# Two state buffers, the last batch's outputs ahead of the first early GLU products, and feature loads on two queues at the end of an S5 mixer

## The reference

```
bu = einsum('blgp,gnp->blgn', u, b_bar)            # 64 groups of 16 channels, 64 complex states each
_, states = associative_scan(..., (a_seq, bu))     # x_t = Abar x_{t-1} + Bbar u_t
y = real(einsum('blgn,gpn->blgp', states, c_mat)) + d * u
g = gelu(y.reshape(bsz, length, D_MODEL))
return (g @ w_glu_a) * sigmoid(g @ w_glu_b)
```

## Time and profile before

| | |
|---|---|
| median of 3 runs | 1217.22 us (1213.07 to 1218.24) |
| profiled execution | 1218.4 us |
| its span in the trace | 1215.6 us |
| mean granted PE clock | 0.969 of full speed |
| PE busy | 1149.1 us, 95% of the span |
| DVE, ACT, POOL busy | 566.5, 410.0, 199.9 us |

### The profile page before, as it was taken

One profiled execution on the slowest core, in us unless ns is written; L12 is line 12 of the kernel. 1 busy time (PEld: TensorE's weight loads), 2 busy tenths in 40 slices (PEclk: granted clock), 3 DMA queues, 4 the chain that ended last, 5 costly groups with the idle time before them and its releaser, 6 DMA issues.

```text
span 1215.6 us, 20049 instructions
## 1 busy us (share of the span) xinstructions
PE 1149.1 (95%) x8147; PEld 1027.3 (85%) x8147; DVE 566.5 (47%) x833; ACT 410.0 (34%) x698; POOL 199.9 (16%) x181
## 2 busy tenths in 40 slices
PE   4488889999999999999999989999999999999997
PEld 4376789999999999999999866668888888888886
DVE  5788743554344333334444345545443433444443
ACT  5723222332222222223332355543332322323332
POOL 3989700002111211100000000000211112110000
PEclk9997679999999999999999999989999999999999
DMA  7224332232223232222223311113233332323222
GB/s 133 73 61 104 85 88 93 82 105 70 90 84 104 69 103 88 76 70 95 95 89 110 110 48 36 36 35 104 76 97 104 104 95 79 102 74 95 95 96 90
DMA packets 119384, 104.58 MB, mean 86 GB/s; under 512 B 21868, under 2 KB 117216, under 8 KB 119008
## 3 DMA queue, kind: packets, MB, share of 16 engines
q1 hardware_dynamic: 108968, 99.58, 26.9%
q10 hardware_dynamic: 10368, 4.33, 1.5%
HBM read 98.11 MB, written 5.24 MB: 85 GB/s over the span
## 4 chain that ended last, share of the span: by engine, by line
issue 43%; PE 43%; POOL 6%; DVE 4%; ACT 1%; DMA 1%; SPq 0%; ACTq 0%; POOLq 0%; DVEq 0%
PE banks L1267 39%; POOL gate L551 2%; PE banks L1384 1%; PE banks L1379 1%; DMA raw_c_re<-in_ssm_c_re 1%; ACT u_row L608 1%; POOL read L513 0%; POOL read L508 0%; POOL read L510 0%; POOL read_t L512 0%; POOL read L511 0%; POOL read_t L509 0%; POOL turn L494 0%; PE banks L1341 0%; PE banks L1328 0%
## 5 line engine op out<-in xcount | busy, mean ns | idle before, releaser
L573 ACT CAST w_high<-raw 128x1024 fp32r<-128x1024 f32 x188 | 197.1, 1049 | 587.2 <-PE banks L1267 587.2
L872 DVE TENSOR_TENSOR w_low<-raw,w_high 128x1024 fp32r<-128x1024 f32 x188 | 230.6, 1227 | 215.2 <-ACT w_high L573 215.0
L1267 PE MATMUL banks<-x_high,w_high 128*128 128x512 f32 (+2 forms) x1184 | 321.8, 324 | 1.0 <-DVE x_low L1082 1.0
L1267 PE MATMUL banks<-x_high,w_low 128*128 128x512 f32 (+2 forms) x1184 | 319.5, 323 | 0.0
L1267 PE MATMUL banks<-x_low,w_high 128*128 128x512 f32 (+2 forms) x1184 | 318.3, 322 | 0.0
L1267 PEld LDWEIGHTS banks<-x_high,w_high 128*128 128x128 f32 x1184 | 199.8, 190 | 19.6 <-issue 2.0
L1267 PEld LDWEIGHTS banks<-x_low,w_high 128*128 128x128 f32 x1184 | 199.6, 189 | 16.2
L1267 PEld LDWEIGHTS banks<-x_high,w_low 128*128 128x128 f32 x1184 | 198.8, 189 | 16.5
L551 POOL TENSOR_TENSOR gate<-gate,rstd_row 128x528 f32<-128x528 f32 (+1 forms) x44 | 79.2, 1800 | 391.5 <-ACT gate L752 391.5
L1267 PE MATMUL banks<-a_high,w_high 128*128 128x256 f32 (+2 forms) x528 | 140.4, 320 | 0.0
L1267 PE MATMUL banks<-a_high,w_low 128*128 128x256 f32 (+2 forms) x528 | 140.2, 320 | 0.0
(11 more groups left out here) (268 smaller groups left out, 1227.4 us busy)
## 6 DMA issues: line engine op xcount, KB each, us to landing
raw<-in_ffn_w_gate SPq DMA_DIRECT2D x22, 1024.0 KB, 5.3
raw<-in_ffn_w_up SPq DMA_DIRECT2D x22, 1024.0 KB, 5.3
raw<-in_ffn_w_down SPq DMA_DIRECT2D x16, 768.0 KB, 4.3
raw<-in_ffn_w_down SPq DMA_DIRECT2D x16, 640.0 KB, 4.1
raw<-in_attn_w_qkv SPq DMA_DIRECT2D x6, 1024.0 KB, 5.0
raw<-in_ssm_w_glu_b SPq DMA_DIRECT2D x4, 1024.0 KB, 5.1
raw<-in_ssm_w_glu_a SPq DMA_DIRECT2D x4, 1024.0 KB, 5.5
k_toep<-k_dram SPq DMA_DIRECT2D x64, 64.0 KB, 2.2
```

The lines of the kernel that those rows point to most:

```text
L573: nc.scalar.copy(w_high[:, j], raw[:, slot, :, j * P:(j + 1) * P]).then_inc(w_rounded, 1)
L872: nc.vector.tensor_tensor(w_low[:, j], raw[:, slot, :, j * P:(j + 1) * P], w_high[:, j], ALU.subtract).then_inc(w_split, 1)
L1267: ins = nc.tensor.matmul(banks[:, bank + h, b0:b0 + cn], w[:, j, k, :], xx[:, first_k + k, c0 + base:c0 + base + cn], start=start and k == ...
```

## The change

`state` gets two buffers, used in turn, and DVE waits for the outputs of two batches ago in place of those of the last one. `outputs(7)` comes directly behind `outputs(6)` in PE's program; `early_glu(0)` comes behind it. Of the eight loads that bring back the last batch's features, ACT issues four and SP the other four. SP's four stand between the two loads of the second set of GLU weights (`i == 1`), and wait for the last store (`y_stored`) and for the `y_feat` buffer to be free (`gt_split`).

```
-        state = sb("state", [P, 2, PB, CS], scope=s5)
+        state = sb("state", [P, 2, 2, PB, CS], scope=s5)
...
                 load_tile(i, 0, by_rows(w_glu_b[0])[:, :, 2 * P * i:2 * P * (i + 1)], wait=i > 0)
+                if i == 1:
+                    b = BATCHES - 1
+                    sp.wait_ge(y_stored, 16 * BATCHES)
+                    sp.wait_ge(gt_split, b - 1)
+                    for g in range(GB // 2, GB):
+                        sp.dma_start(y_feat[g * GROUP:(g + 1) * GROUP, b % 2],
+                                     y_dram[b, :, :, g, :].rearrange("s q c -> q s c")).then_inc(y_placed, 16)
                 load_tile(i, 1, by_rows(w_glu_a[0])[:, :, 2 * P * i:2 * P * (i + 1)], wait=i > 0)
...
-                for g in range(GB):
+                for g in range(GB if b < BATCHES - 1 else GB // 2):
                     nc.scalar.dma_start(y_feat[g * GROUP:(g + 1) * GROUP, b % 2],
...
-                v, cross, out = state_banks(), zt[:].rearrange("p i r c -> p i (r c)"), state[:].rearrange("p i r c -> p i (r c)")
+                v, cross, out = state_banks(), zt[:].rearrange("p i r c -> p i (r c)"), state[:, b % 2].rearrange("p i r c -> p i (r c)")
...
-                if b >= 1:
-                    dve.wait_ge(y_ready, b)
+                if b >= 2:
+                    dve.wait_ge(y_ready, b - 1)
...
-                                                   state[hs, i, r_, :], start=False, stop=i == 1)
+                                                   state[hs, b % 2, i, r_, :], start=False, stop=i == 1)
...
                     injection(b + 1)
                     lags(b + 1)
                     additions(b + 1)
-                else:
-                    early_glu(0)
                 outputs(b)
+            early_glu(0)
             pe.wait_ge(state_ready, BATCHES)
             early_glu(1)
```

## The result

The changed kernel takes 1219.03 us in the median of 20 runs (1216.16 to 1222.76), the kernel before 1216.60 us in 20 (1213.07 to 1219.15). The ratio is 1.0020, with a 95% interval of 1.0011 to 1.0029: slower by 2.4 us (1.3 to 3.5). The prediction had +2.5 us and 1219.7 us. Of the executions behind the ratios further down two are left out, one of the kernel before at 1247.82 us (mean granted clock 0.883) and one of the version with the state ahead of the splits at 1610.46 us (0.665). The profiled execution of the changed kernel has a span of 1215.9 us, 0.3 us above that of before. Two single executions say less here than the medians: between block 2 and the end there are 1029.6 us after (1215.9 - 186.34) and 1034.0 us before (1215.6 - 181.56).

The account below looks back on a forecast made before the run. PE, busy for 95% of the span, was taken as the bound. +1.0 + 2.3 - 0.3 + 0 - 0.5 = +2.5 us gave 1220.9 us profiled, 1219.7 us for the median; range 1213.5 to 1224.5 us.

Parts of the forecast that it names:

- The state buffers: DVE's wait before writing `state` in the mixer goes, 5.6 us in all; worth 0, with bounds of 0 and -0.25 us.
- The wait ahead of `outputs(7)`: Between `outputs(6)` and `outputs(7)` PE idles for state 7, ready at 160.46: 3.5 us of PE time lost.
- `outputs(7)` at the low clock: Behind the idle gap `outputs(7)` takes 8.41 us and ends at 168.9, +1.0 us; other bound 4.67 us.
- 42 pairs: GLU products between `outputs(7)` and `k` = 7, 24 before: 11.8 us (10.3 to 12.0), 3.5 us low; `k` = 7 at 180.7.
- The data: Batch 7's data for `k` = 7 is ready at 176.4, 4.3 us before PE needs it; the two queues are worth nothing.
- Block 2: PE's start of GLU block 2, behind `k` = 7 and 3.16 us of sigmoid, cast and split: 184.6, +3.0 us.
- The clock term: Low clock in block 2 loses 0.9 us (0 to 1.7), where it lost 1.4 before: -0.5 us.
- the clock rising within `outputs(7)`: Rival: `outputs(7)` is low for 3.9 us, then fast, ending at 166.9; -1 us with the clock term, 1216.2 us; chance 0.14.
- the clock that doesn't come back: Rival: the 42 pairs all run low, 18.5 us; block 2 at 191.9, +10.3 us, about 1227 us; chance 0.06.
- late data: Rival: SP's loads, issued beside ACT's, land late, beyond the 4.3 us cover before `k` = 7; about 1220 to 1222 us; chance 0.06.

Follow-up runs that it names:

- the version with the state ahead of the splits: The full change with DVE's splits of the first two weight blocks moved behind the last batch's state: ratio 1.0000, 0.0 us against the kernel before.
- the twice-done `k`: The full change with `k` = 0 to 3 of the first GLU product also done, thrown away, between `outputs(6)` and `outputs(7)`: 1.0000, 0.0 us against before.
- the version that was clearly faster: The full change with state 7 before the weight splits, last Toeplitz blocks and gelu early on ACT, early products of blocks 0 and 1 interleaved: 0.9964, -4.4 us against before.
- the old order with buffers and queues: The full change with `early_glu(0)` put back ahead of `outputs(7)`, two state buffers and two queues kept: 0.9975, -3.0 us against the kernel before.

## Why the prediction was right

The direction, the size and the place were right: PE runs dry ahead of `outputs(7)` and is the bound from there. Step by step:

- *The state buffers.* Costed at 0, with a bound of -0.25 us. Their time alone, -1.3 us (-3.3 to +0.6), doesn't tell 0 from the bound, but at POOL the bound was too narrow: the trace has -1.7 us. It counted only POOL's wait of 0.25 us, and not the 0.84 us at 120.48, which is of the same kind and went too. In the full change they gave nothing: POOL's stretch was 74.5 us, not 73.6.
- *The wait ahead of `outputs(7)`.* Predicted 3.5 us, measured 7.42 in the trace. The size differs by the end of `outputs(6)`, which is early when the clock is high. The end of the wait, which is what counts, was predicted at 160.5 and came at 161.15. `k_toep` was expected at 157.3 and landed at 159.4; it doesn't bind only because the state is later still.
- *`outputs(7)` at the low clock.* 8.41 us predicted, 8.38 measured; it ended at 169.5, not 168.9. Here the Trainium skill ("TensorE: Matmul & The Clock Gate", Part 1) has sustained work release the low clock. The seven microseconds at 0.50 with PE busy throughout, from 162 to 169, again don't bear that out for these matmuls; the products of the twice-done `k` do bear it out.
- *42 pairs.* 11.8 us predicted, 12.95 measured (169.53 to 182.48), since the clock stayed low for 5.7 us and not 3.5; my bound of 12.0 was too tight.
- *The data.* Predicted 4.3 us ahead of PE, measured 5.2. The two queues are hidden in the full change, as said. Where PE waits for the data, the prediction gave them up to 1.84 us; the trace of the queues alone has 1.56 us, and its time, -1.5 us, doesn't exclude zero.
- *Block 2.* Predicted at 184.6, measured at 186.34, +4.8 us against before in these two traces. The clock term behind it was put at -0.5 us and was -1.4, since the clock didn't fall: the windows from 176 to 183 and from 186 to 195 us have 1.00. In the prediction's own terms the trace has +1.6 (end of `outputs(7)`) + 3.5 (42 pairs) - 0.3 - 1.4 (clock) = +3.4 us, where the sum had +1.0 + 2.3 - 0.3 - 0.5 = +2.5; the times give 2.4 (1.3 to 3.5). That the sum hit the median so closely is partly luck: each term was off by 0.6 to 1.2 us, two of them one way and one the other, and one trace's clock pattern isn't the mean of them.

Of the rivals, the clock rising within `outputs(7)`, the clock that doesn't come back, and late data are all absent from the trace.

## What to carry to other kernels

Before moving a step up in an engine's program, read when its inputs are ready, and what the work that it jumps over was covering: here the 18 pairs of products were free filling for a state that came no sooner. Removing a wait shows the next one, and there were three in a row ahead of the same step (state, Toeplitz blocks, gelu). Taking the first two away and shrinking PE's idle time there from 7.4 to about 1 us left the kernel level with the one before (-0.6 us, -1.9 to +0.7), with `outputs(7)` still at the low clock; the version that was clearly faster also filled PE's idle time ahead of block 2. An edit worth nothing in one order may be worth 1.5 us in another, so test the parts of a change alone.

## What the runs showed of the hardware

- `outputs(7)`, 48 small matmuls without a gap (64 or 128 rows by 65 or 66 columns), took 8.3 to 8.4 us at 0.50 granted in all seven traces where PE stood idle for 0.8 to 9.7 us directly ahead of it, and 4.6 to 4.7 us at 1.00 in all five where it stood directly behind products. In `outputs(6)` the clock changed while PE was busy: in the full change it was 1.00 to 151, 0.71 from 151 to 152 and 0.50 from 152 to 153; in the old order with buffers and queues it rose from 0.50 (144 to 147) to 1.00 (148 to 150).
- Products that began at the low clock brought it back 2.4 to 5.7 us after their start (buffers alone and the full change are the ends of that range).
- Useless products in PE's idle time left the kernel level with the one before (0.0 us, -2.4 to +2.3), and by the ratios 2.4 us faster than the version that stood idle, with intervals that overlap.
- The last of eight loads of 64 KB landed 2.1 to 2.3 us after its issue began in six traces, although a load of 1 MB was issued directly behind it on the same queue. It took 4.1 to 4.2 us in the four traces where a store of 264 KB had been issued on the other queue 0.6 to 0.7 us before.
